# Other start addresses for three of the four weight slots and their two views

## The reference, cut to what matters

```python
h = rms_norm(x, attn_norm)
q_r, k_r, v_r, g_r, q_m, k_m, v_m = split(h @ w_in)      # 1024 -> 6144 columns
o_r = group_norm(retention(rotary(q_r), rotary(k_r), v_r)) * silu(g_r)
o_m = causal_softmax_attention(rms_norm(q_m), rms_norm(k_m), v_m)
gate_ret, gate_moba = sigmoid(h @ w_gate + b_gate)
x = x + (gate_ret * (o_r @ w_ret_o) + gate_moba * (o_m @ w_moba_o)) @ w_out
h = rms_norm(x, ffn_norm)
u_gate, u_val = causal_conv3(h @ w_up)                   # 1024 -> 2 x 2816
x = x + (silu(u_gate) * u_val) @ w_down                  # 2816 -> 1024
```

## Time and profile before

| | us |
|---|---|
| median of 3 runs | 469.83 (469.77 to 469.90) |
| the profiled execution | 470.34 |
| its span, first to last instruction | 468.6 |
| PE busy | 462.3 (99%) |
| DVE busy | 300.7 (64%) |
| ACT busy | 254.6 (54%) |
| POOL busy | 19.6 (4%) |

### The profile page before, as it was taken

How to read it: one execution, slowest core, us unless ns; L and a number is a source line. 1 busy time by engine, 2 the same in 40 slices (tenths; PEclk the granted TensorE clock), 3 DMA queues, 4 the chain that set the end, 5 groups by cost and what they waited for, 6 DMA issues and landing times.

```text
span 468.6 us, 7797 instructions
## 1 busy us (share of the span) xinstructions
PE 462.3 (99%) x3123; PEld 425.5 (91%) x3123; DVE 300.7 (64%) x366; ACT 254.6 (54%) x362; POOL 19.6 (4%) x27
## 2 busy tenths in 40 slices
PE   8999999999999999999999999999999999999997
PEld 5689999888888999999999788999999999988886
DVE  4797883764665556445338676688778888884313
ACT  5775442146784739361445355877777766763300
POOL 0210000311110001000000000000000000000000
PEclk9999999999999999999999999999999999999999
DMA  7997444243445533943453733625555555538002
GB/s 278 423 400 271 180 180 181 90 159 151 151 168 191 218 131 106 389 140 141 167 190 141 268 136 130 239 75 231 201 193 191 195 199 189 204 134 322 0 1 90
DMA packets 14122, 87.20 MB, mean 186 GB/s; under 512 B 1552, under 2 KB 2192, under 8 KB 4496
## 3 DMA queue, kind: packets, MB, share of 16 engines
q1 hardware_dynamic: 13680, 85.25, 48.5%
q0 software_dynamic: 416, 1.57, 1.0%
HBM read 85.77 MB, written 1.05 MB: 185 GB/s over the span
## 4 chain that ended last, share of the span: by engine, by line
PE 92%; DVE 3%; DMA 2%; ACT 1%; SPq 1%; issue 0%; ACTq 0%
PE bank L377 17%; PE bank L379 17%; PE bank L378 17%; PE bank L342 5%; PE bank L344 5%; PE bank L343 5%; PE bank L624 4%; PE bank L627 4%; PE bank L625 4%; PE bank L398 2%; PE bank L530 2%; DMA w_raw<-weights_dram 2%; PE bank L532 2%; PE bank L531 2%; DVE w_pair L921 2%; ACT w_pair L644 1%
## 5 line engine op out<-in xcount | busy, mean ns | idle before, releaser
L921 DVE TENSOR_TENSOR w_pair<-w_raw,w_pair 128x2048 fp32r<-128x2048 f32 x75 | 170.5, 2289 | 81.9 <-ACT w_pair L644 81.7
L377 PE MATMUL bank<-h_hi,w_pair 128*128 128x256 f32 x576 | 161.7, 281 | 0.0
L378 PE MATMUL bank<-h_lo,w_pair 128*128 128x256 f32 x576 | 160.9, 279 | 0.0
L644 ACT ACTIVATE w_pair<-w_raw 128x2048 fp32r<-128x2048 f32 x75 | 142.0, 1919 | 34.5 <-PE bank L627 17.1
L379 PE MATMUL bank<-h_hi,w_pair 128*128 128x256 f32 x576 | 160.6, 279 | 0.0
L377 PEld LDWEIGHTS bank<-h_hi,w_pair 128*128 128x128 f32 x576 | 108.2, 188 | 0.4 <-issue 0.4
L378 PEld LDWEIGHTS bank<-h_lo,w_pair 128*128 128x128 f32 x576 | 108.3, 188 | 0.1
L379 PEld LDWEIGHTS bank<-h_hi,w_pair 128*128 128x128 f32 x576 | 108.3, 188 | 0.0
L1184 DVE SCALAR_TENSOR_TENSOR area<-area,col 128x256 f32<-128x256 f32 x88 | 37.8, 482 | 16.7 <-ACT area L847 14.1
L342 PE MATMUL bank<-w_pair,h_hi 128*128 128x512 f32 x96 | 37.9, 395 | 0.0
L344 PE MATMUL bank<-w_pair,h_lo 128*128 128x512 f32 x96 | 37.4, 390 | 0.0
(11 more groups left out here) (139 smaller groups left out, 572.0 us busy)
## 6 DMA issues: line engine op xcount, KB each, us to landing
w_raw<-weights_dram SPq DMA_DIRECT2D x75, 1024.0 KB, 4.9
w_raw<-weights_dram SPq DMA_DIRECT2D x3, 512.0 KB, 7.7
ys<-x_dram SPq DMA_DIRECT2D x2, 512.0 KB, 13.1
xs<-x_dram POOLq DMA_DIRECT2D x1, 1024.0 KB, 8.1
area<-decay_dram SPq DMA_DIRECT2D x1, 768.0 KB, 13.5
out_dram<-ys SPq DMA_DIRECT2D x3, 256.0 KB, 2.0
w_raw<-weights_dram SPq DMA_DIRECT2D x2, 256.0 KB, 4.1
xs<-x_chan_dram SPq DMA_DIRECT2D x1, 512.0 KB, 6.0
```

Source lines behind the costliest of these rows:

```text
L377: mm(o, s_hi, r_hi[:, k, :], start=(k == 0 and m % 2 == 0), stop=False)
L378: mm(o, s_hi, r_lo[:, k, :], start=False, stop=False)
L644: A(w_parts(n, r)[0], raw[r][:, :], ACT.Copy).then_inc(hi_ready, 1)
L921: tt(lo, raw[r][:, :], hi.bitcast(f32), ALU.subtract).then_inc(lo_ready, 1)
```

## The change

The constant `SHIFT` is replaced by four numbers of spare elements, one for each slot: 8, 16, 0 and 0 (32, 64, 0 and 0 bytes). The token-type view of slot r begins that far into `w_pair{r}`. The small tensors between the slots are put in another order, so slots 1 to 3 begin elsewhere. No instruction changes but for its addresses.

```diff
--- before.py
+++ after.py
@@ -18,7 +18,7 @@
 BLOCK_COLS = 512
 HALF_ELEMS = 2048
 SLOTS = 4
-SHIFT = 8
+VIEW_SPARE = (8, 16, 0, 0)
 UP_COLS = 256
 UP_BLOCKS = D_FF // UP_COLS
 DOWN_HALVES = D_FF // P // 2
@@ -80,20 +80,20 @@
         a_lo = sb("a_lo", [P, D_FF // P, SEQ], f32r)
         gn_stats = sb("gn_stats", [P, 8, 6])
         ss_x = sb("ss_x", [P, 2])
-        w_pair0 = sb("w_pair0", [P, SHIFT + 2 * HALF_ELEMS], f32r)
+        w_pair0 = sb("w_pair0", [P, VIEW_SPARE[0] + 2 * HALF_ELEMS], f32r)
         ss_qk = sb("ss_qk", [P, 4, 8])
+        gn_rstd = sb("gn_rstd", [P, 8])
+        w_pair1 = sb("w_pair1", [P, VIEW_SPARE[1] + 2 * HALF_ELEMS], f32r)
+        inv_qk = sb("inv_qk", [P, 4, 8])
+        w_pair2 = sb("w_pair2", [P, VIEW_SPARE[2] + 2 * HALF_ELEMS], f32r)
         row_max = sb("row_max", [P, 16])
-        gn_rstd = sb("gn_rstd", [P, 8])
-        w_pair1 = sb("w_pair1", [P, SHIFT + 2 * HALF_ELEMS], f32r)
-        inv_qk = sb("inv_qk", [P, 4, 8])
         neg_max = sb("neg_max", [P, 16])
+        row_sum = sb("row_sum", [P, 16])
+        w_pair3 = sb("w_pair3", [P, VIEW_SPARE[3] + 2 * HALF_ELEMS], f32r)
         neg_half = sb("neg_half", [P, 8])
-        w_pair2 = sb("w_pair2", [P, SHIFT + 2 * HALF_ELEMS], f32r)
-        row_sum = sb("row_sum", [P, 16])
         inv_sum = sb("inv_sum", [P, 16])
         gn_mv = sb("gn_mv", [P, 8, 2])
         ss_x2 = sb("ss_x2", [P, 4])
-        w_pair3 = sb("w_pair3", [P, SHIFT + 2 * HALF_ELEMS], f32r)
         inv_x2 = sb("inv_x2", [P, 2])
         area = sb("area", [P, 8192])
         x_head = sb("xs", [P, 2 * KT + 2048])
@@ -226,7 +226,7 @@
                 moving = n // 2 in TOKEN_BLOCKS or n >= DOWN_FIRST_HALF + 2
             else:
                 moving = False
-            first = SHIFT if moving else 0
+            first = VIEW_SPARE[r] if moving else 0
             return [w_pair[r][:, first + HALF_ELEMS * i:first + HALF_ELEMS * i + HALF_ELEMS] for i in range(2)]
 
         block = ctx.enter_context(nc.Block())
```

## The result

| | before | after |
|---|---|---|
| median | 469.80 us (4 runs, 469.73 to 469.90) | 476.18 us (4 runs, 476.01 to 476.25) |
| ratio | | 1.0132 (95% interval 1.0121 to 1.0144) |
| profiled execution, its span | 470.34, 468.6 | 476.23, 474.4 |
| PE busy | 462.3 | 468.3 |

The kernel became 6.4 us slower. The forecast was 478.8 with a range of 471.0 to 485.0, so direction and range hold and the size was too large by 2.6 us. The sum was less good than its total: its channel-type terms were too large by about 5 us and its token-type terms too small by about 3, and the two errors partly cancelled.

The account below looks back on a forecast made before the run. TensorE's matmul issue pace was taken as the bound. Terms 5.28 + 3.52 + 1.12 - 0.16 - 0.56 - 0.24 = +8.96 us on the profiled 470.34 gave 479.3, 478.8 us for the median; range 471.0 to 485.0.

Parts of the forecast that it names:

- What bounds the kernel: Whole kernel: the end is set by how fast TensorE issues matmuls; PE is busy 462.3 of 468.6 us.
- That the distance between the two operands counts: All matmuls: surplus time set by moving start minus stationary start, modulo 256 bytes; chance 0.45 with its bounds.
- The rival by which start addresses do nothing: Down halves 66 and 67 are slow for their own reason; the change does nothing, 469.8 us; chance 0.08.
- That the width doesn't count: All matmuls: surplus is the same at 256 and 512 columns, 20.0 ns at distance 7, 13.3 at 0, 10.0 at 1.
- channel, slot 3: Channel-type matmuls of slot 3, distance 1 to 7: +10.0 ns on each of 528, +5.28 us.
- halves of 6.08 us: Sign in the up loop: slot 3's halves of 48 matmuls take 6.08 us; keeping 5.60 would make the forecast wrong.
- Distances 3 and 5 at 256 columns: Channel-type matmuls of slots 1 and 2: surplus taken as 13.3 ns, +3.52 us, bounds 0 to +10.56.
- Token-type, slot 1: Token-type halves of slot 1, distance 0 to 7: +6.67 ns a matmul in 7 halves, +1.12 us.
- Token-type, slots 2 and 3: Token-type halves at distances 3 and 1: 0 and -0.56 us; down halves 66 and 67 gain 0.16 and 0.24.
- The terms at 0: Splits on ACT and DVE, small statistics tensors and shifted DMAs: each 0, the last store with 0.1 us either way.
- Odd or even: Rival: only odd or even distance counts, with width; channel halves unchanged, token halves +3.36 us, 473.2 us; chance 0.28.
- Farther apart is free: Rival: reads disturb only within one or two steps; distances 3 and 5 near 2.1 ns, -5.05 us, 464.8; chance 0.14.

Follow-up runs that it names:

- the kernel of the widths: Kernel before with token-type distance 0 in slots 0 and 1, 7 in 2 and 3, down halves 68 to 75 cut narrower: 478.04 us (one run).

## Why the prediction was right, and where it was not

**What bounds the kernel: right.** PE's pace is the time. The whole difference is in starts of matmuls, none of it in waits, and the splits on ACT and DVE saw nothing of the addresses: VectorE's took 2269 to 2294 ns after, against the earlier trace rows.

**That the distance between the two operands counts: right.** The kernel that moves everything by 32 bytes is unchanged to 0.1%, while a move of one operand against the other by as much costs 6.7 ns a matmul of 512 columns. The rival by which start addresses do nothing is out, as the trace of before had made likely. By the rule of the Trainium skill ("TensorE: Matmul & The Clock Gate", section "Step-by-step: what each phase is for") that the two read ports don't take from each other the change would have cost nothing; it measured +1.3%.

**That the width doesn't count: wrong, and this is the step that failed.** I took it from distance 0, the only one measured at both widths in the trace of before, where the surplus is 13.3 at both. It is the exception. At distance 7 it is 20.0 at 512 columns and 11.6 at 256. So the term "channel, slot 3" was about seven times too large: priced from a row of the other width at +10.0 ns a matmul and +5.28 us, it measured +1.6 ns and +0.7 us. The sign that I had named for it, halves of 6.08 us, did not come; they took 5.68, nearer to the 5.60 by which the forecast was to be wrong.

**Distances 3 and 5 at 256 columns: half right.** I took 13.3 ns for both. Distance 3 has 13.3; distance 5 has 10.6, or 11.9 in some halves. The term of +3.52 us measured 1.52 + 0.45.

**Token-type, slot 1: right.** +1.12 us predicted, +1.1 measured: same distance and same width as the row that priced it. It was the one term with a row that matched in both.

**Token-type, slots 2 and 3: wrong in sign for slot 3.** I expected 226.7 and 223.3 ns and both run at 233.3; 0 and -0.56 us became +1.0 and +0.9, and halves 66 and 67 gained nothing. For slot 3 the cause is the same step: the price of distance 1 came from 256 columns. For slot 2 it is the 13.3 ns that I had interpolated for distance 3.

**The terms at 0: right.** The splits kept their times, and from the first matmul of half 76 to the end of the span it is 8.2 us before and 8.3 after, so the shifted stores cost no more than the 0.1 us allowed. One detail of a reading was wrong without consequence: modulo 32 steps the channel-type distances of before are 25, 17, 9 and 1; 7, 15, 23 and 31 are the same with the other sign.

**The rivals.** Odd or even had the token-type part right, 3.36 us against 3.2 measured alone, and would have been nearer than mine for it. It missed that channel-type halves would change at all (3.1 us), and its idea falls with the even distances: 229 to 233.3 ns at 512 columns, 113.3 to 120.0 at 256. Farther apart is free: distance 4 is slow at both widths. Its bound of 2.1 ns for the surplus was never reached; the lowest is 6.7. The transposes that gave it move 128 columns, and the split products cut to 128 columns took 112 ns as well, so their 108.8 ns may not be a surplus over the columns at all; no run separates this.

**The total: in part luck.** Against the two kernels with one part each, the channel-type part of my sum was over by 5.3 us and the token-type part under by 2.6. Only because they cancel did the forecast miss by 2.6 us; the odd-or-even rival, at 473.2, missed by 3.0.

**What the trace of before already held and I passed over:** The earlier trace rows show two paces, 5.65 and 5.60 us, at one distance. I took them as one price of 116.7 to 117.7 ns with a range. They were the mark of the two phases, without which the kernels at distances 2 and 6 can't be understood.

**What stays open.** Why the surplus has these values for these distances. Which of the two paces a stretch takes. With one distance in all slots it is kept until another shape intervenes. The distances don't decide it: halves 4 to 11 at distance 1 ran at 117.8 ns in the trace of before and at 116.7 with everything 32 bytes higher. And neither a slot of distance 1 nor a half at distance 0 in front sets the fast one. Single executions of the kernel with distance 2 spread over 1.7 us, which would fit with different choices in different executions, but only one of them was profiled. A kernel with all channel-type halves at 113.3 ns would come to about 463 us, by the sum in the expectation for distance 2; none of these reached it.

## What to carry to other kernels

Price a matmul stream by a row that agrees in width and in distance of its operands; a price taken over from the other width was wrong here by a factor of about seven. In this kernel, where TensorE is the bound and each matmul loads its own stationary operand, the start of the moving operand relative to the stationary one, modulo 256 bytes, was worth 7 ns of 113 to 120 at 256 columns and 7 of 227 to 234 at 512, and it cost nothing to choose: 0 for 512 columns with 6 steps of 32 bytes for 256 made it 1.0% faster, with 2 steps 0.6%. Read it from differences of start times over a whole half, for the durations printed beside them overlap.

## What the runs showed of the hardware that I had not expected

- No rule as simple as odd or even fits. At 512 columns only distance 0 (226.7 ns) and, less so, 2 (229) stand out from 231.4 to 236.5 everywhere else that was tried; at 256 columns only 2 and 6 (113.3).
- Two stable paces for one and the same stream, 113.3 and 117.8 ns: at distance 2 the first was kept for 19 halves of 48 matmuls in a row (47 to 65), the second for 9 (31 to 39). At distance 1 they are 116.7 and 117.8.
- The exchange of roles changed nothing: 120.0 and 118.3 ns at distances 0 and 7 whether the weights or the activations are the moving operand.
- A matmul of 128 columns behind its own load of a 128 x 128 stationary operand took about 112 ns from start to start in the kernel of the widths, hardly less than one of 256 columns at its best (113.3).
